# Chunk mask of the latent scores inside the contraction, and half as many mask columns for the differential scores

## The chip, the cores and the metric

The kernel runs on one core of one Trainium2 chip. The metric is the device time of one execution in microseconds. An execution is compared with others by the median of several runs.

## The reference

Two layers of a streaming encoder are run for a prompt (512 new frames) and for samples (8 streams of 16 new frames with 256 cached ones). Layer 0 has two groups of heads side by side, latent attention and differential attention; layer 1 has stick-breaking attention. Both head groups of layer 0 use the same chunk-causal mask: a frame sees all frames of its own chunk of 64 and of the chunks before.

```python
CHUNK = 64

def _chunk_mask(qpos, kpos):
    return (kpos[None, :] // CHUNK) <= (qpos[:, None] // CHUNK)

def _mla_core(q_abs, q_rope, ckv, krope, qpos, kpos):
    s = (einsum('bqhc,bkc->bhqk', q_abs, ckv) + einsum('bqhr,bkr->bhqk', q_rope, krope)).astype(float32)
    s = jnp.where(_chunk_mask(qpos, kpos), s * (MLA_QK_DIM ** -0.5), NEG_INF)
    p = jax.nn.softmax(s, axis=-1).astype(ckv.dtype)
    return jnp.einsum('bhqk,bkc->bqhc', p, ckv)

def _diff_core(q, k, v, qpos, kpos, lam):
    s = jnp.einsum('bqhid,bkhid->bhiqk', q, k).astype(jnp.float32) * (DIFF_HD ** -0.5)
    s = jnp.where(_chunk_mask(qpos, kpos), s, NEG_INF)
    p = jax.nn.softmax(s, axis=-1)
    a = (p[:, :, 0] - lam * p[:, :, 1]).astype(v.dtype)
    return jnp.einsum('bhqk,bkhe->bqhe', a, v)
```

## The kernel before

The prompt's 512 frames are four tiles of 128 rows, the samples are a fifth tile. All matrix products with the large weights are made of three products of split operands (a high and a low part). The weights come in quarters of 256 KB from SP's queue into a ring of three stages (`load_quarter`, L727); ScalarE writes the high part (`w_hi`, L1368), VectorE the low part (`w_lo`, L1598), and TensorE takes a quarter when both are there. SP issues the load of quarter n + 3 when quarter n has been split.

The order of the work is one list of jobs, `make_schedule`, written out by hand. Each engine runs through the same list and does its own part of each job; semaphores join them. A job that TensorE writes to PSUM takes a bank from a ring, and waits until the bank's last use has been read.

Behind the first projections comes the job `rms`: POOL and VectorE norm the latents, and POOL then issues the stores of the new latents and rotary keys: first those of the samples (L889, L890), then, when these have landed, those of the prompt (L892, L893). SP waits for the samples' stores and loads their latents back (L753). At this time the projection of the values `dv` is under way; SP, ScalarE and VectorE handle its weight quarters.

Then follow 48 steps of softmax attention: 16 latent steps ("M", tile t of the queries, pair of heads), 8 latent sample steps ("MS"), 16 differential steps ("D", tile t, head) and 8 differential sample steps ("DS"). Tile t of the queries sees key tiles 0 to t, so a score has 128, 256, 384 or 512 columns. A step makes two score maps side by side in two banks (`pair`); VectorE takes their row maxima (`peak`, L1699), ScalarE the exponential (L1448), VectorE the weights (L1720). Two steps later TensorE transposes the weights (`turn`, `turn2`), ScalarE and VectorE copy the result (L1469, L1735), and another step later TensorE makes the product with the values. Between these parts stand pieces of the next projections (`dk`, `dq` and so on) and, ahead of a sample's score, the transposes of its cache (`cacheT`, L1059 and L1061, copied by VectorE in L1690 and L1691).

In a latent step the contraction of a score runs over 96 rows: 64 rows that are the head's own and 32 rotary ones. Queries lie in `qT`, which is the memory of `x_sb` (the profile gives it that name), keys in `mlaK`. A fp32 product of TensorE appears as two matmuls. After the two scores, two bf16 matmuls add the mask to the last 128 columns of each map: the stationary operand is the unit matrix, the moving one is `mask_chunk`, with -1e30 where the key's chunk is a later one. The differential steps do the same. All tiles of 128 keys below the last one are fully visible, so only the last tile needs a mask; in it the rows of the first chunk must not see the second chunk's 64 columns.

```python
for i in range(2):
    h = 2 * pair + i
    mm(o[:, i, 0:n], qT[0:QK, h, tok(t)], mlaK[0:QK, h, 0:n], True, False)
for i in range(2):
    m = mm(o[:, i, n - P:n], identb[:, :], mask_chunk[:, :], False, True)
m.then_inc(done, 1)
```

Of the kernel before, what the change touches and what calls it, by code (L numbers as in the profile page):

```python
# [25 lines left out]
BF16 = mybir.dt.bfloat16  # L26
# [4 lines left out]
P = 128  # L31
# [13 lines left out]
EPS = 1e-5  # L45
MH, NOPE, ROT, MV = 8, 64, 32, 64
QK = NOPE + ROT
QL, KVL = 256, 128
SEC_A = QL + KVL + ROT
DH, HD, DROT = 4, 64, 16  # L50
# [364 lines left out]
def trunk_kernel(nc, a, out):  # L415
# [9 lines left out]
    def sem(name):  # L425
        return ctx.enter_context(nc.semaphore(name))
# [4 lines left out]
    with ctx:  # L431

        def sb(name, shape, dt=F32):
            return alloc(ctx, name, shape, dt)
# [10 lines left out]
        latT = work8[:, :, :].rearrange("p a b -> p (a b)")[:, 0:3 * TOK].rearrange("p (a b) -> p a b", a=3)  # L445
        ident = sb("ident", [P])
        identb = sb("identb", [P], BF16)
        mask_chunk = sb("mask_chunk", [P], BF16)
        mask_causal = sb("mask_causal", [P], BF16)
        mask_new = sb("mask_new", [NEW], BF16)  # L450
        peak = sb("peak", [8, 2])
# [102 lines left out]
        hi_done, cvt_done = sem("hi_done"), sem("cvt_done")  # L554
        pool_cvt_done = sem("pool_cvt_done")
        xhi_done = sem("xhi_done")
        upper_read = sem("upper_read")
        subln_done = sem("subln_done")
        ocvt_hi, ocvt_done = sem("ocvt_hi"), sem("ocvt_done")
# [305 lines left out]
        def _(pool):  # L865
# [17 lines left out]
            for job in schedule:  # L883
                kind = job[0]
                if kind == "rms":
                    pool.wait_ge(pow_in, pow_no[job])
                    nc.gpsimd.tensor_tensor(ss[:, 2, :], ss[:, 1, :], minus_half[:, :], ALU.pow).then_inc(pow_out, 1)
                    pool.wait_ge(rms_done, 1)
                    pool.dma_start(ckv_s, lat[:, S_TILE, QL:QL + KVL]).then_inc(stored_ckv, 16)  # L889
                    pool.dma_start(kr_s, lat[:, S_TILE, QL + KVL:]).then_inc(stored_ckv, 16)  # L890
                    pool.wait_ge(stored_ckv, 32)
                    pool.dma_start(ckv_p, lat[:, 0:PT_TILES, QL:QL + KVL]).then_inc(stored_ckv, 16)  # L892
                    pool.dma_start(kr_p, lat[:, 0:PT_TILES, QL + KVL:]).then_inc(stored_ckv, 16)  # L893
                elif kind == "dk":
                    _, t, half = job
                    n = rot_no[job]
                    pool.wait_ge(rot_done, n)
                    pool.dma_start((dk_p[t] if t < PT_TILES else dk_s)[:, half * HALF:(half + 1) * HALF],
                                   rot[:, (n - 1) % 4, :]).then_inc(stored_rot[(n - 1) % 4], 16)
                elif kind == "dv" and job[2] == 1:  # L900
                    t = job[1]
                    wait_drained(pool, ("dv", t, 0))
                    wait_drained(pool, job)
                    if t < PT_TILES:
                        outputs += 16
                        pool.dma_start(dv_p[t], dv[:, t, :]).then_inc(stored, 16)
                    else:
                        pool.dma_start(dv_s, dv[:, t, :]).then_inc(stored_dv, 16)
                elif kind == "post":
                    pool.wait_ge(pow_in, pow_no[job])  # L910
                    sums = sums_of(job[1])
                    nc.gpsimd.tensor_tensor(ss[:, 2, sums], ss[:, 1, sums], minus_half[:, 0:DH], ALU.pow).then_inc(pow_out, 1)
                elif kind == "cvt" and job[1] in POOL_SPLITS:
                    n = job[1]
                    sec, words = n // QUARTERS, slice(n % QUARTERS * 512, (n % QUARTERS + 1) * 512)
                    pool.wait_ge(hi_done, n + 1)
                    nc.gpsimd.tensor_tensor(w_lo[:, sec % 2, words], stage[:, n % STAGES, :],
                                            w_hi[:, sec % 2, words].bitcast(F32), ALU.subtract).then_inc(pool_cvt_done, 1)
                elif kind == "ln":
                    i = ln_no[job] % 2  # L920
                    pool.wait_ge(pow_in, pow_no[job])
                    if ln_no[job] > 2:
                        n = ln_no[job] - 2
                        pool.wait_ge(ln_done, n)
                    nc.gpsimd.tensor_tensor(rstd[:, i, :], mv[:, i, 1:2], minus_half[:, 0:1], ALU.pow).then_inc(pow_out, 1)  # L925
                elif kind in ("k", "v"):
                    _, g, t = job
                    wait_drained(pool, job)
                    cols = slice(g * GW, (g + 1) * GW)
                    k_out, v_out = (sk_p[t], sv_p[t]) if t < PT_TILES else (sk_s, sv_s)  # L930
                    if kind == "k":
                        slot = (kn_no[job] - 1) % 2
                        pool.dma_start(k_out[:, cols], k_n[:, slot, :]).then_inc(stored_kn[slot], 16)
                    else:
                        pool.dma_start(v_out[:, cols], v_n[:, g % 2, t, :]).then_inc(
                            stored_vn[g % 2] if t < PT_TILES else stored_v[g], 16)
# [13 lines left out]
        def _(pe):  # L950
# [45 lines left out]
            for job in schedule:  # L996
# [76 lines left out]
                elif kind == "score":  # L1073
# [4 lines left out]
                    if s[0] == "M":  # L1078
                        _, t, pair = s
                        pe.wait_ge(kr_done, PT_TILES)  # L1080
                        for j in range(4):
                            wait_drained(pe, ("latT", j))
                        for i in range(2):
# [1 line left out]
                            wait_drained(pe, ("qT", t, i))  # L1085
                        for i in range(2):
                            h = 2 * pair + i
                            mm(o[:, i, 0:n], qT[0:QK, h, tok(t)], mlaK[0:QK, h, 0:n], True, False)
                        for i in range(2):
                            m = mm(o[:, i, n - P:n], identb[:, :], mask_chunk[:, :], False, True)  # L1090
                        m.then_inc(done, 1)
                    elif s[0] == "MS":
                        b = s[1]
# [9 lines left out]
                    elif s[0] == "D":  # L1103
# [5 lines left out]
                            r = slice(HD * i, HD * i + HD)  # L1109
                            mm(o[:, i, 0:n], dqT[t][r, h, :], dkT[r, h, 0:n], True, False)  # L1110
                        for i in range(2):
                            m = mm(o[:, i, n - P:n], identb[:, :], mask_chunk[:, :], False, True)
                        m.then_inc(done, 1)
                    elif s[0] == "DS":
                        b = s[1]
# [451 lines left out]
        def _(dve):  # L1567
# [17 lines left out]
            for job in schedule:  # L1585
# [42 lines left out]
                elif kind == "lam":  # L1628
# [2 lines left out]

                    dve.wait_ge(consts_in, 16)
                    v.tensor_copy(identb[:, :], ident[:, :])
                    v.tensor_copy(mask_chunk[:, :], probs[:, 0, 0:P])
                    v.tensor_copy(mask_causal[:, :], probs[:, 0, P:2 * P])
                    v.tensor_copy(mask_new[:, :], probs[:, 0, 2 * P:MASKS])
                    link(v.tensor_tensor(lam4[:, 0:2, :], lam4[:, 0:2, :], lam4[:, 2:4, :], ALU.mult))
# [274 lines left out]
def shape_constants():  # L1912
# [1 line left out]
    r = np.arange(P)  # L1914
    neg = np.float32(-1e30)
    masks = np.zeros((P, MASKS), np.float32)
    masks[:, 0:P] = np.where(r[None, :] // 64 <= r[:, None] // 64, 0, neg)
    masks[:, P:2 * P] = np.where(r[None, :] < r[:, None], 0, neg)
    masks[:, 2 * P:] = np.where(r[None, :NEW] < r[:, None] % NEW, 0, neg)
    sel = ((r[:, None] // QUAD == r[None, :] // QUAD) & (r[:, None] % NEW == r[None, :] % NEW)).astype(np.float32)  # L1920
    second = r // NEW % 2
    sign = np.stack([1 - second, second], 1).astype(np.float32)
    pos = np.concatenate([np.arange(SEQ), PAST + r % NEW]).astype(np.float32)

    def rope(rot, theta):
# [3 lines left out]
        both = np.stack([np.cos(ang), np.cos(ang), -np.sin(ang), np.sin(ang)], 1).astype(np.float32)  # L1929
        return np.ascontiguousarray(both.reshape(TILES, P, 2, 2, half).transpose(1, 0, 2, 3, 4))  # L1930

    return {"c_ident": np.eye(P, dtype=np.float32), "c_masks": masks, "c_sel": sel, "c_sign": sign,
            "c_ropem": rope(ROT, 10000.0), "c_roped": rope(DROT, 500000.0)}


# [14 lines left out]
```

## Time and profile before

| | |
|---|---|
| median of 3 runs | 857.05 us (856.89 to 857.83) |
| the profiled execution's own time | 856.7 us |
| its span, first to last instruction | 854.9 us |
| TensorE (PE) busy, matmuls | 826.6 us, 97% |
| VectorE (DVE) busy | 524.8 us, 61% |
| ScalarE (ACT) busy | 412.8 us, 48% |
| GpSimd (POOL) busy | 74.8 us, 9% |
| TensorE's share of the chain that ended last | 81% |
| DMA, mean over the span | 101 GB/s |

Busy time counts the time in which an engine has at least one instruction running; matmuls overlap one another, so that the time from one start to the next says more than a matmul's duration. The chain that ended last is followed back from the last instruction, at each step to what released it. Loads of weights onto TensorE are a row of their own (PEld). A row of a view in order of time merges like instructions that follow one another: start, time from the first start to the last end, engine, line, operation, what is written and read, shapes, count, and in brackets the idle time before and who ended it. Since a window cuts such merges, a row's count can be that of a part.

### The profile page before, as it was taken

The page shows a single profiled execution, that of the slowest core. Times are in us where ns is not written, and L with a number is a line of the kernel's source. Part 1 is how long each engine was busy: PE and PEld are TensorE (multiplying, and loading weights), DVE is VectorE, ACT ScalarE, POOL GpSimd, SP SyncE. Part 2 cuts the span into 40 slices and gives each one's busy share as a digit, 9 for nine tenths or more (in the row PEclk, how much of TensorE's full clock was granted, in tenths as well). Part 3 has the DMA queues.
Part 4 walks back from the last instruction along what each step waited for, and adds up shares of the span by engine and source line. Part 5 has one row for each costly group of instructions (what it writes and reads, how often), then busy time and mean ns, then how long its engine had stood idle before and what let it go on. Part 6 is the DMA issues. An engine that isn't in the chain of part 4 may idle for free.

```text
span 854.9 us, 17106 instructions
## 1 busy us (share of the span) xinstructions
PE 826.6 (97%) x6676; PEld 706.4 (83%) x6676; DVE 524.8 (61%) x1048; ACT 412.8 (48%) x945; POOL 74.8 (9%) x102
## 2 busy tenths in 40 slices
PE   7999999999999999999999999999999999999995
PEld 6996688888888888768899998889888878887674
DVE  4175346655565647756942465666666766778777
ACT  4333433334354455532234556675566665687710
POOL 3020001000000000000220011001100110121002
PEclk9999999999999999999999999999999999999998
DMA  7631211211332334414133334233332433334113
GB/s 236 153 98 51 62 44 57 64 44 38 96 99 88 109 108 138 152 51 148 56 113 105 119 106 130 87 92 125 122 99 79 136 114 116 122 119 146 52 38 123
DMA packets 67534, 86.25 MB, mean 101 GB/s; under 512 B 6017, under 2 KB 53921, under 8 KB 67457
## 3 DMA queue, kind: packets, MB, share of 16 engines
q1 hardware_dynamic: 63712, 74.47, 28.4%
q0 software_dynamic: 3744, 10.70, 4.0%
q8 instruction: 55, 0.90, 0.4%
q14 instruction: 23, 0.18, 0.1%
HBM read 74.25 MB, written 10.90 MB: 100 GB/s over the span
## 4 chain that ended last, share of the span: by engine, by line
PE 81%; issue 9%; DVE 4%; ACT 4%; POOL 2%; DMA 0%; DVEq 0%; SPq 0%; POOLq 0%; ACTq 0%
PE turn L952 24%; PE pair L952 17%; PE value L952 16%; PE proj L952 15%; PE turn L992 3%; PE turn L1168 2%; POOL rstd L925 1%; PE value L992 1%; PE proj L992 1%; PE proj L1168 1%; DVE w_lo L1598 1%; ACT w_hi L1368 1%; PE pair L992 1%; DVE probs L1710 0%; PE value L1168 0%
## 5 line engine op out<-in xcount | busy, mean ns | idle before, releaser
L1598 DVE TENSOR_TENSOR w_lo<-stage,w_hi 128x512 fp32r<-128x512 f32 (+1 forms) x136 | 91.9, 683 | 118.2 <-ACT w_hi L1368 117.8
L952 PE MATMUL turn<-w_hi,xT_hi 128*128 128x256 f32 (+2 forms) x340 | 106.0, 312 | 0.9 <-DVE xT_lo L1603 0.6
L952 PE MATMUL turn<-w_hi,xT_lo 128*128 128x256 f32 (+2 forms) x340 | 102.5, 301 | 0.0
L952 PE MATMUL turn<-w_lo,xT_hi 128*128 128x256 f32 (+2 forms) x340 | 102.4, 301 | 0.0
L1368 ACT CAST w_hi<-stage 128x512 fp32r<-128x512 f32 (+1 forms) x144 | 87.4, 616 | 20.6 <-PE value L952 6.4
L952 PEld LDWEIGHTS turn<-w_hi,xT_hi 128*128 128x128 f32 x340 | 64.8, 191 | 3.6 <-DVE x_sb L1840 1.4
L952 PEld LDWEIGHTS turn<-w_hi,xT_lo 128*128 128x128 f32 x340 | 64.8, 191 | 2.4
L952 PEld LDWEIGHTS turn<-w_lo,xT_hi 128*128 128x128 f32 x340 | 64.9, 191 | 2.1
L1710 DVE TENSOR_TENSOR_SCAN probs<-probs 128x512 f32<-128x512 f32 (+4 forms) x80 | 61.5, 801 | 1.7
L1448 ACT ACTIVATE work<-pair,peak 128x512 f32<-128x512 f32 (+4 forms) x80 | 40.9, 516 | 44.5 <-DVE peak L1699 44.4
L952 PE MATMUL value<-w_hi,xT_hi 128*128 128x256 f32 (+2 forms) x194 | 60.5, 312 | 0.4 <-DVE w_lo L1598 0.4
L952 PE MATMUL value<-w_lo,xT_hi 128*128 128x256 f32 (+2 forms) x194 | 57.7, 297 | 0.0
L952 PE MATMUL value<-w_hi,xT_lo 128*128 128x256 f32 (+2 forms) x194 | 57.6, 297 | 0.0
L952 PE MATMUL proj<-w_hi,xT_hi 128*128 128x256 f32 (+2 forms) x186 | 56.1, 302 | 0.3
L952 PE MATMUL proj<-w_hi,xT_lo 128*128 128x256 f32 (+2 forms) x186 | 54.4, 293 | 0.0
L952 PE MATMUL proj<-w_lo,xT_hi 128*128 128x256 f32 (+2 forms) x186 | 54.4, 292 | 0.0
L952 PE MATMUL pair<-w_hi,xT_hi 128*128 128x256 f32 (+2 forms) x160 | 53.0, 331 | 0.1
L952 PE MATMUL pair<-w_hi,xT_lo 128*128 128x256 f32 (+2 forms) x160 | 52.0, 325 | 0.0
L952 PE MATMUL pair<-w_lo,xT_hi 128*128 128x256 f32 (+2 forms) x160 | 52.0, 325 | 0.0
L952 PE MATMUL turn<-xT_hi,w_hi 128*128 128x320 f32 x160 | 50.9, 318 | 0.0
L952 PE MATMUL turn<-xT_hi,w_lo 128*128 128x320 f32 x160 | 49.4, 309 | 0.0
L952 PE MATMUL turn<-xT_lo,w_hi 128*128 128x320 f32 x160 | 49.4, 309 | 0.0
(528 smaller groups left out, 2079.1 us busy)
## 6 DMA issues: line engine op xcount, KB each, us to landing
stage<-in_w_in_odd_dram SPq DMA_DIRECT2D x64, 256.0 KB, 2.7
stage<-in_w_in_even_dram SPq DMA_DIRECT2D x44, 256.0 KB, 2.8
k_c<-in_cache_sb_k_dram SPq DMA_DIRECT2D x32, 256.0 KB, 3.4
v_c<-in_cache_sb_v_dram SPq DMA_DIRECT2D x32, 256.0 KB, 2.9
mlaK<-in_cache_diff_k_dram SPq DMA_DIRECT2D x8, 512.0 KB, 4.1
mlaK<-in_cache_diff_v_dram SPq DMA_DIRECT2D x8, 512.0 KB, 4.3
stage<-in_w_out_even_dram SPq DMA_DIRECT2D x16, 256.0 KB, 2.6
stage<-in_w_out_odd_dram SPq DMA_DIRECT2D x16, 256.0 KB, 2.6
```

The source lines that it names most:

```text
L925: nc.gpsimd.tensor_tensor(rstd[:, i, :], mv[:, i, 1:2], minus_half[:, 0:1], ALU.pow).then_inc(pow_out, 1)
L952: return nc.tensor.matmul(o, l, r, start=first, stop=last)
L992: i = nc.tensor.transpose(ps(job)[0:c, c0:c0 + r], src, ident[0:r, 0:r])
L1168: m = nc.tensor.transpose(ps(job)[0:kn, j * P:(j + 1) * P], p[:, k0:k0 + kn], ident[:, :])
L1368: nc.scalar.copy(piece(w_hi[:, sec % 2, k * 512:(k + 1) * 512]), piece(stage[:, n % STAGES, :])).then_inc(hi_done, 1)
L1448: e = nc.scalar.activation(prob(s, i), ps(score)[:, i, 0:width(s)], ACT.Exp, bias=peak[:, r, i:i + 1], accum_out=total[:, r, i:i + 1])
L1598: v.tensor_tensor(piece(w_lo[:, sec % 2, words]), piece(stage[:, n % STAGES, :]), piece(w_hi[:, sec % 2, words].bitcast(F32)), ALU.subtrac ...
L1710: i = v.tensor_tensor_scan(c, c, c, 0.0, ALU.add, ALU.max)
```

## The change

The mask of the latent scores moves into the contraction. Eight rows are added to queries and keys, one for each chunk of the prompt: row c of the queries is 1 where the query's own chunk comes before chunk c, row c of the keys is -1e30 where the key lies in chunk c. Their product is -1e30 exactly where the key's chunk is a later one. The rows are constants (`c_chunks`, 2 x 8 x 512 words in DRAM) and are loaded on POOL's queue into partitions 96 to 103 of `qT` and `mlaK`, the same for all eight heads. The two mask matmuls of a latent step are gone, and each latent score waits for `chunks_in`.

The differential steps keep their two mask matmuls, which now add only the last 64 columns of the mask to the last 64 columns of the map; the 64 columns before them held zeros only.

```diff
+CHUNK = 64
+CHUNKS = SEQ // CHUNK
+QKM = QK + CHUNKS
...
-        mask_chunk = sb("mask_chunk", [P], BF16)
+        mask_chunk = sb("mask_chunk", [CHUNK], BF16)
...
+        chunks_in = sem("chunks_in")
...
                     pool.wait_ge(rms_done, 1)
+                    for i, rows in enumerate((qT[QK:QKM, :, 0:SEQ], mlaK[QK:QKM, :, :])):
+                        pool.dma_start(rows, a["c_chunks"][i].unsqueeze(1).broadcast_to([CHUNKS, MH, SEQ])).then_inc(chunks_in, 16)
                     pool.dma_start(ckv_s, lat[:, S_TILE, QL:QL + KVL]).then_inc(stored_ckv, 16)
...
                         pe.wait_ge(kr_done, PT_TILES)
+                        pe.wait_ge(chunks_in, 32)
...
                         for i in range(2):
                             h = 2 * pair + i
-                            mm(o[:, i, 0:n], qT[0:QK, h, tok(t)], mlaK[0:QK, h, 0:n], True, False)
-                        for i in range(2):
-                            m = mm(o[:, i, n - P:n], identb[:, :], mask_chunk[:, :], False, True)
+                            m = mm(o[:, i, 0:n], qT[0:QKM, h, tok(t)], mlaK[0:QKM, h, 0:n], True, True)
                         m.then_inc(done, 1)
...
                             mm(o[:, i, 0:n], dqT[t][r, h, :], dkT[r, h, 0:n], True, False)
                         for i in range(2):
-                            m = mm(o[:, i, n - P:n], identb[:, :], mask_chunk[:, :], False, True)
+                            m = mm(o[:, i, n - CHUNK:n], identb[:, :], mask_chunk[:, :], False, True)
...
-                    v.tensor_copy(mask_chunk[:, :], probs[:, 0, 0:P])
+                    v.tensor_copy(mask_chunk[:, :], probs[:, 0, P - CHUNK:P])
...
+    own, chunk = np.arange(SEQ)[None, :] // CHUNK, np.arange(CHUNKS)[:, None]
+    chunks = np.stack([np.where(own < chunk, 1, 0), np.where(own == chunk, neg, 0)]).astype(np.float32)
```

POOL's order at the job `rms`, before (`lat` holds the latents, `dv` the values):

```order
L887 TENSOR_TENSOR ss<-ss,minus_half 128x10 [waits pow_in]
L889 DMA out_dram<-lat 128x128 [waits rms_done]
L890 DMA out_dram<-lat 128x32
L892 DMA out_dram<-lat 128x4x128 [waits stored_ckv]
L893 DMA out_dram<-lat 128x4x32
```

and with the change:

```order
L891 TENSOR_TENSOR ss<-ss,minus_half 128x10 [waits pow_in]
L894 DMA x_sb<-in_c_chunks_dram 8x8x512 [waits rms_done]
L894 DMA mlaK<-in_c_chunks_dram 8x8x512
L895 DMA out_dram<-lat 128x128
L896 DMA out_dram<-lat 128x32
L898 DMA out_dram<-lat 128x4x128 [waits stored_ckv]
L899 DMA out_dram<-lat 128x4x32
```

Two DMAs stand ahead of the stores; nothing else of POOL's order moves.

TensorE's order at a latent step on tile 0 (`ckv_c` and `kr_c` are a sample's cache, `vm` the values), before:

```order
L1059 MATMUL value<-ident,ckv_c 128x128
L1061 MATMUL value<-ident,kr_c 96x128 x2
L952 MATMUL pair<-mlaK,x_sb 128x128 [waits drained_score0,drained_score1,drained_proj0,drained_turn0,drained_value0,drained_turn2,drained_turn1,kr_done,drained_pair1]
L952 MATMUL pair<-mlaK,x_sb 128x128
L952 MATMUL pair<-mask_chunk,identb 128x128 x2
L952 MATMUL proj<-probs,vm 64x128 [waits drained_proj0,drained_turn1,drained_value0]
L952 MATMUL proj<-probs,vm 64x128
```

and with the change:

```order
L1065 MATMUL value<-ident,ckv_c 128x128
L1067 MATMUL value<-ident,kr_c 96x128 x2
L958 MATMUL pair<-mlaK,x_sb 128x128 [waits drained_score0,drained_proj0,drained_score1,drained_value0,drained_turn0,drained_turn1,drained_turn2,chunks_in,kr_done,drained_pair1]
L958 MATMUL pair<-mlaK,x_sb 128x128
L958 MATMUL proj<-probs,vm 64x128 [waits drained_proj0,drained_turn1,drained_value0]
L958 MATMUL proj<-probs,vm 64x128
```

The mask's row is gone in each of the 16 latent steps, and each waits for `chunks_in` besides. In the differential steps the row stays and reads 128x64.

## Rows read from the trace of the kernel before

**Rows 1.** The page: busy us (share) x instructions; the chain that ended last by engine.
```profile
PE 826.6 (97%) x6676; PEld 706.4 (83%) x6676; DVE 524.8 (61%) x1048; ACT 412.8 (48%) x945; POOL 74.8 (9%) x102
...
PE 81%; issue 9%; DVE 4%; ACT 4%; POOL 2%; DMA 0%; DVEq 0%; SPq 0%; POOLq 0%; ACTq 0%
```

**Rows 2.** Stretches: us, busy PE PEld DVE ACT POOL (x), granted clock, DMA share, GB/s.
```profile
100.00:150.00 50.00, 48.19 (x345) 39.05 (x344) 24.63 (x71) 19.68 (x55) 3.78 (x7) 1.00 0.18 50
150.00:200.00 50.00, 49.31 (x373) 41.05 (x372) 29.04 (x84) 19.11 (x61) 1.62 (x3) 1.00 0.19 52
```

**Rows 3.** Instructions on mask_chunk: duration min/median/max, first and last start.
```profile
L952 PEld LDWEIGHTS pair<-mask_chunk,identb x64: 95/98/100, 105.4 to 371.5; 128*128 128x128 bf16 x64
L952 PE MATMUL pair<-mask_chunk,identb x64: 217/220/230, 105.8 to 371.5; 128*128 128x128 bf16 x64
```

**Rows 4.** TensorE in order of time: start us, us, what; a latent step, tile 2.
```profile
155.91 1.46 PE L952 MATMUL pair<-mlaK,x_sb 96*128 96x384 f32 x4
157.21 0.28 PE L952 MATMUL pair<-mask_chunk,identb 128*128 128x128 bf16 x2
157.41 1.09 PE L952 MATMUL value<-probs,vm 128*64 128x128 f32 x16
```

**Rows 5.** The same view where a narrow product follows transposes with no mask.
```profile
665.99 0.63 PE L992 MATMUL value<-ident,k_c 128*128 128x128 f32 x4
666.46 0.27 PE L992 MATMUL proj<-ident,oval 128*128 128x128 f32 x1
666.66 0.88 PE L952 MATMUL turn<-work,v_n 128*64 128x128 f32 x12
```

**Rows 6.** The same view of VectorE and TensorE, a latent step on tile 0.
```profile
148.67 0.42 DVE L1691 COPY lat<-value 32x256 f32<-32x256 f32 x1
...
147.25 0.28 PE L952 MATMUL pair<-mask_chunk,identb 128*128 128x128 bf16 x2
...
149.19 0.67 PE L952 MATMUL pair<-lat,w_uq 128*128 128x256 f32 x2 [0.38 <-issue]
```

**Rows 7.** The same view behind the first latent step on tile 2.
```profile
123.27 0.44 PE L952 MATMUL value<-probs,vm 128*64 128x128 f32 x4 [0.36 <-DVE probs L1735]
```

**Rows 8.** The same view, differential steps: the next product with 64, with 128 columns.
```profile
242.77 0.29 PE L952 MATMUL pair<-mask_chunk,identb 128*128 128x128 bf16 x2
242.99 0.66 PE L952 MATMUL value<-probs,vm 128*64 128x128 f32 x8
...
281.80 0.28 PE L952 MATMUL pair<-mask_chunk,identb 128*128 128x128 bf16 x2
281.92 1.11 PE L952 MATMUL value<-dv,probs 128*128 128x128 f32 x8
```

**Rows 9.** The same view of POOL, SP, ScalarE, VectorE and TensorE, 56 to 61 us.
```profile
56.02 0.62 POOL L889 DMA_DIRECT2D out_dram<-lat  x1 [5.77 <-DVE lat L1582]
...
56.35 4.61 SPq L727 DMA_DIRECT2D stage<-in_w_in_even_dram  x4
...
59.22 0.62 ACT L1368 CAST w_hi<-stage 128x512 fp32r<-128x512 f32 x1 [2.44 <-DMA stage<-in_w_in_even_dram]
...
59.88 0.69 DVE L1598 TENSOR_TENSOR w_lo<-stage,w_hi 128x512 fp32r<-128x512 f32 x1 [2.35 <-ACT w_hi L1368]
...
60.62 0.39 PE L952 MATMUL pair<-w_hi,xT_hi 128*128 128x256 f32 x1
```

**Rows 10.** DMA issues of the whole run: count, KB each, median us to landing.
```profile
stage<-in_w_in_even_dram SPq DMA_DIRECT2D x44, 256.0 KB, 2.8
...
ropem<-in_c_ropem_dram POOLq DMA_DIRECT2D x1, 160.0 KB, 2.5
...
g_q<-in_q_norm_g_dram POOLq DMA_DIRECT2D x1, 128.0 KB, 4.0
```

**Rows 11.** DMA queues and issues from 20 to 26 us.
```profile
q0 software_dynamic: 146, 0.38, 98.1%
...
stage<-in_w_in_even_dram SPq DMA_DIRECT2D x2, 256.0 KB, 10.4
```

More of the change, by code:

```diff
@@ L1916, in shape_constants @@
     masks = np.zeros((P, MASKS), np.float32)
-    masks[:, 0:P] = np.where(r[None, :] // 64 <= r[:, None] // 64, 0, neg)
+    masks[:, 0:P] = np.where(r[None, :] // CHUNK <= r[:, None] // CHUNK, 0, neg)
     masks[:, P:2 * P] = np.where(r[None, :] < r[:, None], 0, neg)
@@ L1930, in rope @@
         return np.ascontiguousarray(both.reshape(TILES, P, 2, 2, half).transpose(1, 0, 2, 3, 4))
-    return {"c_ident": np.eye(P, dtype=np.float32), "c_masks": masks, "c_sel": sel, "c_sign": sign,
+    return {"c_ident": np.eye(P, dtype=np.float32), "c_masks": masks, "c_chunks": chunks, "c_sel": sel, "c_sign": sign,
             "c_ropem": rope(ROT, 10000.0), "c_roped": rope(DROT, 500000.0)}
```

## The prediction

> **What bounds the kernel now.** I read the page first, then the stretch table, the mask's own instructions, and then short stretches of the order in time around one step of each kind. TensorE is busy for 97% of the span and carries 81% of the chain that ended last [rows 1]. In the stretches that hold most latent steps it is busy for 48.2 of 50 us, then 49.3 of 50, and its clock is granted in full [rows 2]. So time taken off TensorE there is time off the end, except just ahead of a place where TensorE waits for something that did not depend on it. Those exceptions decide this change. A difference under 0.2% (1.7 us) I count as no change, about what a measurement of this kernel can tell.
>
> **Part 1: the mask matmuls of the latent scores go.** There are 64 mask matmuls, 32 of them in the 16 latent steps [rows 3]. In a latent step the first mask matmul starts at 157.21 and the value product behind it at 157.41 [rows 4]: the pair costs 0.20 us from start to start. Not all of that comes back. The value product holds only 64 stationary columns, and where such a product follows a transpose with no mask between them, it starts 0.20 us after it (666.46 to 666.66) [rows 5], while the transposes ahead of it start about 0.12 us apart (four in 0.63 us, of which 0.27 is the last one's own time). So 0.09 us of the 0.20 is a price of the change of shape that stays, and a removed pair is worth 0.11 us. The bound above is 0.20, if the change of shape hides under the long score matmul.
>
> Where does the 0.11 us reach the end? Of a latent step on a query tile 3 or 2 the value product follows at once and TensorE goes on. Of a step on tile 0 or 1 it doesn't: between the masks and the next stall there are only a few short products. At 147.25 the masks of such a step run, and at 149.19 the sample's score starts after a wait; the last thing to come is VectorE's copy of the cache transposes, which ends at 149.09 [rows 6]. VectorE comes to it after a rotation and a weight split, and both wait for ScalarE's work on the projection before. All of that hangs on the projection that TensorE finished before the score, not on the masks. A TensorE that arrives 0.11 us sooner waits 0.11 us longer. I find such a stall behind seven of the eight steps on tiles 0 and 1; behind the eighth the copy ends about 0.1 us ahead of TensorE, which is no gain either. The first step on tile 2 is the same: its value product starts at 123.27 after 0.36 us idle that a copy on VectorE ended [rows 7]. That leaves seven of sixteen steps: 7 x 0.11 = 0.8 us. The bound above is 7 x 0.20 = 1.4.
>
> The eight added rows of the contraction cost nothing on TensorE: the stationary and moving columns stay as they are, and the four score matmuls of 384 columns start 0.32 us apart (1.30 us to the first mask) [rows 4], which is their columns twice at 2.4 GHz, and rows don't enter. Nor does the new wait at the first latent score, whose masks run at 105.8 us [rows 3]: its transfers are issued at about 56 us [rows 9], and weight quarters in the thickest traffic of the start landed in 10.4 us [rows 11].
>
> **Part 2: 64 mask columns in place of 128 for the differential scores.** All 32 mask matmuls stay, half as wide. Two of them last 0.28 us together where one lasts 0.22 [rows 3, 8], so the second starts 0.06 us after the first. Before a value product with 64 stationary columns the pair takes 0.22 us up to the next start (242.77 to 242.99), before one with 128 only 0.12 (281.80 to 281.92) [rows 8]. In the second case the next product's weights are what is late: its eight matmuls take 1.11 us with the last one's 0.27, so 0.84 for seven steps of 0.11, and the extra is the first weight load that the short mask cannot cover. There a narrower second mask brings nothing. Five of the sixteen steps are of the first kind. At least 5 x 0.03 = 0.15 us is gained, at most 16 x 0.06 = 1.0 (each mask costs half). I take 0.35, nearer the lower end, because weight loads of 0.10 us already stand behind each mask [rows 3]. The Trainium skill (TensorE: Matmul & The Clock Gate, section "Back-to-back issue gap") puts the floor of a matmul with up to 64 columns at about 25 ns; by it the first mask of each pair would fall from 0.06 to 0.03 us and the sum would gain 16 x 0.03 = 0.5 in place of 0.35. No row here has such a mask.
>
> VectorE's copy of the mask is one short instruction that gets half as long; it stands off the path, and I count nothing. The score reductions read the same columns as before.
>
> **Part 3: two DMAs are put ahead of the stores on POOL's queue.** They bring 8 x 8 x 512 words each, 128 KB into eight partitions, every 2 KB row read eight times. POOL would issue them at 56.02 and, 0.62 us later, at 56.64, where it now issues the two sample stores [rows 9]. Those stores move back by 1.2 us, and with them the two prompt stores, which wait for them, and SP's load of the new latents behind its four weight quarters. SP has no further quarter to load for a long while then, and VectorE asks for the prompt stores only at the first cache transposes, behind the first latent score: nothing of this is late.
>
> What is late next is a weight quarter. SP issues four quarters from 56.35 on [rows 9]. The first of them is the last quarter of the second value section. It lands just before 59.22, where ScalarE, idle for 2.44 us on that DMA, converts it; VectorE follows at 59.88 after 2.35 us idle, and TensorE, which reaches the product with this quarter at 60.62, finds it ready with nothing to spare [rows 9]. Behind it on ScalarE stand the four copies of the rotary keys, behind them VectorE's latent copies, and for those TensorE's key products wait. So each microsecond by which this quarter lands later is a microsecond at the end. It shares the DMA engines with the two new transfers, which are issued 0.3 us before it and 0.3 after.
>
> The price of that is in no row of the trace; the nearest bound it. Below: nothing, if they pass on engines that the quarter doesn't need. As ordinary traffic: a load of 160 KB lands in 2.5 us and one of 256 KB in 2.8 [rows 10], 0.3 us for 96 KB, so 256 KB more in the way are 0.8. Above: at the start POOL loads gains and lambdas as rows that all 128 partitions read from one place. In the stretch from 20 to 26 us POOL's queue filled 98.1% of all engines with 0.38 MB, 64 GB/s, and the weight quarters issued then landed after 10.4 us [rows 11]. At that rate 256 KB take 4.1 us. One 128 KB transfer of that kind landed in 4.0 us, a plain one of 160 KB in 2.5 [rows 10], so 1.5 us more for its repeated reads. The new rows are repeated 8 times, not 128, and are read from eight places. I take 1.5 us, nearest to the pair of 128 and 160 KB.
>
> **The sum.** -0.8 (latent masks) - 0.35 (half-wide masks) + 1.5 (the late quarter) = +0.35 us. Against the profiled execution's 856.7 us that is 857.05. The median of the runs shown is 857.05, 0.35 above that execution, so the forecast for the median is 857.4 us: no change that can be measured. With a late quarter of 0.4 to 2.9 us it is 856.3 to 858.8.
>
> **The rivals.**
> *The new transfers clog the engines.* Mechanism: eight partitions and repeated rows make them slow, and the quarter waits behind them. Price: 4.1 us by the start's rate, so 857.05 - 1.15 + 4.1 = 860.0, slower. It decides from 2.9 us on. For it: the idle ScalarE and the 98.1% with 64 GB/s. Against it: few engines may be involved, and the repetition is 8, not 128. The Trainium skill (SBUF — State Buffer, section "Door 1: The DMA port swizzle") says that DMA bandwidth goes with the ports that the partitions reach, and partitions 96 to 103 reach two of sixteen, at some 27 GB/s each. As an estimate from that page the two transfers would take 4.8 us, and if the quarter waited for all of it the time would be 860.7. No row of this trace shows so narrow a large transfer.
>
> *The transfers cost nothing.* Then only the gains are left: 855.9 by my terms, 854.65 with both upper ends (1.4 and 1.0). It is faster by more than 1.7 us only if the masks are worth over 1.7 us, so for most of this case's width it is still no change. For it: the 2.8 us landing is mostly latency.
>
> *The change gives its full count on TensorE.* If the stalls behind the tile 0 and 1 steps shrank too, 16 x 0.11 + 0.5 = 2.3 us would go, and with a quarter that is late by 0.5 us the time is 855.25. Against it: the order in time at 147 to 149 us, where ScalarE and VectorE never wait for a mask.
>
> **How the numbers follow.** The forecast has 0.40, the clog 0.36, free transfers 0.17, the full count 0.07. Of the last two I give 0.17 to faster by over 0.2%, the rest is within it; the clog is all slower but for its lower edge. So faster 0.17, same 0.48, slower 0.35. The range for 8 in 10 goes from 855.0, inside the free case, to 860.0, the clog's own value.
>
> **What would show it.** The mask should have 32 matmuls of 64 columns, and value products should start one score matmul plus 0.09 us after the last score's start. The stalls that now end at 149.19 should be 0.1 us longer. ScalarE's conversion at 59.22 should move to about 60.7, and everything after it until the first latent score with it. The forecast is wrong if that conversion stays where it is and the first latent score still starts at 104 us after the same launch, or if it moves past 62. My split of the gain is wrong if TensorE is more than 1.5 us ahead between the first latent score and 375 us.

## The result and the profile after

The changed kernel takes 861.74 us in the median of 6 runs (861.06 to 862.06), the kernel before, run beside it, 857.44 (856.40 to 859.91). The ratio is 1.0050, 95% interval 1.0040 to 1.0061: slower by 0.5%, 4.3 us. The forecast was 857.4 with a range up to 860.0. The profiled execution took 861.52 us, with a span of 859.7 against 854.9.

The page: busy us by engine, and the chain of waits by engine.
```profile
PE 825.6 (96%) x6644; PEld 704.5 (82%) x6644; DVE 524.6 (61%) x1048; ACT 413.0 (48%) x945; POOL 76.0 (9%) x104
...
PE 78%; issue 9%; DVE 6%; ACT 4%; POOL 2%; DMA 1%; SPq 0%; DVEq 0%; POOLq 0%; ACTq 0%
```
TensorE is busy for 1.0 us less than in [rows 1], and the span is 4.8 us longer: the loss is waiting, and the chain has lost 3% of TensorE for 2% of VectorE and 1% of DMA. The stretch table shows where. The kernel before (columns as in [rows 2]):
```profile
56.00:61.00 5.00, 5.00 (x45) 4.88 (x44) 2.25 (x5) 2.13 (x4) 2.48 (x4) 1.00 0.59 174
61.00:75.00 14.00, 13.92 (x63) 8.21 (x62) 10.06 (x28) 5.71 (x12) 0.74 (x2) 1.00 0.21 64
```
and the changed one:
```profile
56.00:61.00 5.00, 5.00 (x46) 5.00 (x46) 2.17 (x5) 0.37 (x1) 2.36 (x4) 1.00 0.64 89
61.00:75.00 14.00, 9.88 (x30) 5.30 (x28) 8.16 (x24) 6.15 (x10) 2.08 (x3) 0.88 0.50 113
66.00:67.00 1.00, 1.00 (x7) 1.00 (x7) 0.65 (x2) 1.00 (x2) 0.84 (x2) 0.50 0.44 44
```
Between 61 and 75 us TensorE is busy for 9.88 us where it had 13.92, and its clock is granted at 0.88 on average, at 0.50 from 66 to 67 us; in no other stretch up to 600 us does its busy time differ by more than 0.8 us. The order in time, of POOL, SP, ScalarE, VectorE and TensorE:
```profile
56.70 0.64 POOL L894 DMA_DIRECT2D x_sb<-in_c_chunks_dram  x1 [5.78 <-DVE lat L1587]
...
57.03 8.82 SPq L731 DMA_DIRECT2D stage<-in_w_in_even_dram  x4
...
57.34 0.58 POOL L894 DMA_DIRECT2D mlaK<-in_c_chunks_dram  x1
...
57.90 0.60 POOL L895 DMA_DIRECT2D out_dram<-lat  x1
...
64.11 0.62 ACT L1373 CAST w_hi<-stage 128x512 fp32r<-128x512 f32 x1 [6.65 <-DMA stage<-in_w_in_even_dram]
...
64.76 0.69 DVE L1603 TENSOR_TENSOR w_lo<-stage,w_hi 128x512 fp32r<-128x512 f32 x1 [6.55 <-ACT w_hi L1373]
...
65.51 0.58 PE L958 MATMUL pair<-w_hi,xT_hi 128*128 128x256 f32 x1 [4.12 <-DVE w_lo L1603]
...
66.10 0.41 PE L958 MATMUL pair<-w_hi,xT_lo 128*128 128x256 f32 x1
...
66.32 0.41 PE L958 MATMUL pair<-w_hi,xT_hi 128*128 128x256 f32 x1
```
This execution reached POOL's first issue at 56.70, 0.68 us later than [rows 9]; that lateness is there already at VectorE's split of x early in the launch (15.00 against 14.33) and is not the change's. Counted from POOL's first issue, ScalarE's conversion comes 7.41 us later where it came after 3.20: **4.21 us late**. TensorE stood idle for 4.12 us for it. Then it runs its matmuls of 256 columns 0.21 us apart instead of 0.12, the lower of its two clock levels (1.2 GHz) in place of 2.4 GHz. From this first matmul behind the wait to the first one on `work` and `w_uk` it needs 3.89 us in the kernel before and 4.94 in the changed one. The first latent score in the order in time, of the kernel before:
```profile
103.98 1.98 PE L952 MATMUL pair<-mlaK,x_sb 96*128 96x512 f32 x4 [0.70 <-ACT vm L1411]
```
and of the changed one:
```profile
109.91 1.98 PE L958 MATMUL pair<-mlaK,x_sb 104*128 104x512 f32 x4 [0.70 <-ACT vm L1416]
```
From POOL's first issue that is 47.96 us before and 53.21 now, **5.25 us later**: 4.21 of the late quarter, 1.04 at the lower clock. The landings say why (POOL's and SP's issues from 56 to 61 us, median us to landing; in the kernel before the quarters of this stretch had 3.0, of the whole run 2.8 [rows 10]):
```profile
stage<-in_w_in_even_dram SPq DMA_DIRECT2D x3, 256.0 KB, 7.2
x_sb<-in_c_chunks_dram POOLq DMA_DIRECT2D x1, 128.0 KB, 6.4
mlaK<-in_c_chunks_dram POOLq DMA_DIRECT2D x1, 128.0 KB, 7.0
```
The two sample stores behind them were held up as well: 7.2 and 7.4 us to landing.

The gains of the masks are there too. The masks that are left, by their duration in ns:
```profile
L958 PE MATMUL pair<-mask_chunk,identb x32: 193/198/203, 242.1 to 376.1; 128*128 128x64 bf16 x32
```
TensorE in order of time: a stall as [rows 6] showed it at 149.19, a latent step as in [rows 4], and two differential steps as in [rows 8]:
```profile
154.88 0.67 PE L958 MATMUL pair<-lat,w_uq 128*128 128x256 f32 x2 [0.49 <-issue]
...
161.61 1.46 PE L958 MATMUL pair<-mlaK,x_sb 104*128 104x384 f32 x4
162.99 1.09 PE L958 MATMUL value<-probs,vm 128*64 128x128 f32 x16
...
247.81 0.23 PE L958 MATMUL pair<-mask_chunk,identb 128*128 128x64 bf16 x2
247.97 0.66 PE L958 MATMUL value<-probs,vm 128*64 128x128 f32 x8
...
286.71 0.23 PE L958 MATMUL pair<-mask_chunk,identb 128*128 128x64 bf16 x2
286.78 1.14 PE L958 MATMUL value<-dv,probs 128*128 128x128 f32 x8
```
The value product stands 1.38 us behind the first of four score matmuls that are 0.32 us apart: one score and 0.09 us more, as forecast. The stall has 0.49 us idle where it had 0.38: the 0.11 us freed ahead of it is waited away. A differential pair of masks takes 0.16 us up to the next product, and 0.07 where that product has 128 columns. From the first latent score to the first differential one it was 131.97 us and is 131.14 (**-0.83**); from there to the last matmul of the last differential score 135.29 and 134.82 (**-0.47**); behind that to the last matmul nothing changed (0.02 us). 5.25 - 0.83 - 0.47 = 3.95 us; with the 0.68 of the launch that is 4.6 of the 4.8 us between the spans. The medians are 4.3 us apart.

### The profile page after: what moved, and what is told of

Its sections match the earlier page's. It is cut to its first block, busy times and chain, and to the rows that moved or that the text cites. A ratio compares the mean times of both kernels' runs of the same rounds, so it can differ in the third digit from the quotient of the medians.

```text
span 859.7 us, 17046 instructions
## 1 busy us (share of the span) xinstructions
PE 825.6 (96%) x6644; PEld 704.5 (82%) x6644; DVE 524.6 (61%) x1048; ACT 413.0 (48%) x945; POOL 76.0 (9%) x104
## 4 chain that ended last, share of the span: by engine, by line
PE 78%; issue 9%; DVE 6%; ACT 4%; POOL 2%; DMA 1%; SPq 0%; DVEq 0%; POOLq 0%; ACTq 0%
PE turn L958 23%; PE value L958 16%; PE pair L958 15%; PE proj L958 15%; PE turn L998 3%; PE turn L1173 2%; POOL rstd L931 1%; PE value L998 1%; PE proj L998 1%; DMA stage<-in_w_in_even_dram 1%; DVE w_lo L1603 1%; ACT w_hi L1373 1%; PE proj L1173 1%; DMA x_sb<-in_x_prompt_dram 0%; DVE probs L1715 0%
```

## The experiments

Theory A: the loss is the two transfers, by way of one weight quarter and the clock. Theory B: it comes from using the rows (a wait, 104 rows of contraction). Eleven kernels ran: four on where the time goes, seven on when and why the transfers cost. "Late" is counted from POOL's first issue behind the norm (where no row transfer goes first, from the sample store) to ScalarE's conversion and to the first latent score, against 3.20 and 47.96 us in the kernel before.

**The transfers alone, nobody reads them.**
```diff
                     pool.wait_ge(rms_done, 1)
+                    for i, rows in enumerate((qT[QK:QKM, :, 0:SEQ], mlaK[QK:QKM, :, :])):
+                        pool.dma_start(rows, a["c_chunks"][i].unsqueeze(1).broadcast_to([CHUNKS, MH, SEQ])).then_inc(chunks_in, 16)
```


> The kernel before with only the two row transfers added at the changed kernel's place on POOL's queue; the masks stay as matmuls and the rows are read by nobody. Theory A (the transfers hold up the last quarter of the second value section, TensorE stands still for about 4 us, and its clock then falls for a while): slower by 4.5 to 5.5 us against the kernel before, ScalarE's conversion 4 to 5 us later than before (counted from the same point of the launch), a granted clock under 1.00 between 61 and 75 us. Theory B (the loss comes from using the rows: the wait of the first latent score, 104 rows of contraction in place of 96): within 0.5 us of the kernel before.

Measured: 863.44 us, ratio 1.0067 (1.0054 to 1.0080). ScalarE's conversion and TensorE's first matmul behind it, in order of time:
```profile
64.14 0.62 ACT L1375 CAST w_hi<-stage 128x512 fp32r<-128x512 f32 x1 [6.51 <-DMA stage<-in_w_in_even_dram]
...
65.54 0.58 PE L959 MATMUL pair<-w_hi,xT_hi 128*128 128x256 f32 x1 [3.98 <-DVE w_lo L1605]
```
The conversion is 4.06 us late, TensorE idle for 3.98, the first latent score 5.02 late. The transfers by themselves make the whole loss; theory B falls. The time is 5.8 us longer by the ratio, 6.1 by the medians, somewhat over the 4.5 to 5.5 that theory A had.

**The same rows, loaded at three other moments.** Early: ahead of the wait for the norm. Late: behind the first store of differential values. Behind: just behind the two sample stores.
```diff
+                    for i, rows in enumerate(...):            # early
                     pool.wait_ge(rms_done, 1)
-                    for i, rows in enumerate(...):            # as changed
                     pool.dma_start(ckv_s, ...)
                     pool.dma_start(kr_s, ...)
+                    for i, rows in enumerate(...):            # behind
...
                         pool.dma_start(dv_p[t], dv[:, t, :]).then_inc(stored, 16)
+                        if outputs == 16:
+                            for i, rows in enumerate(...):    # late
```


> The changed kernel with the two row transfers issued ahead of POOL's wait for the norm, at about 51 us in place of 56, where the DMA engines of the kernel before are idle. Theory A: the loss goes almost wholly and the gains of the masks (0.8 and 0.4 us) stay: 0.5 to 1.5 us faster than the kernel before; the two transfers alone need some 6 to 7 us, so up to 1 us of the late quarter may be left. Theory B: 3.5 to 4.5 us slower than the kernel before, as the changed kernel is.

> The changed kernel with the two row transfers issued behind the first store of differential values, at about 69 us, with the first latent score at 104 us. Theory A: 1.0 to 1.4 us faster than the kernel before, no idle stretch of TensorE between 56 and 64 us, and the transfers land by 76 us, just as SP issues its next weight quarter. If the next quarters at 76 us are held up, TensorE has some slack there and the time rises by less than 1 us. Theory B: 3.5 to 4.5 us slower than the kernel before.

> The changed kernel with the two row transfers issued behind the two sample stores instead of ahead of them, 1.2 us later, so 0.9 and 1.5 us behind the issue of the weight quarter (which landed 2.8 us after its issue before). If the transfers must be in the engines first to hold it up: the quarter comes 0 to 1.5 us late and the time is at or just under that of the kernel before. If the quarter's own packets come out slowly and share with them to its end: 2 to 4 us late and 1.5 to 3.5 us slower than the kernel before.

Measured: early 856.05 us, ratio 0.9985 (0.9976 to 0.9994); late 856.12, 0.9984 (0.9975 to 0.9993); behind 855.58, 0.9984 (0.9973 to 0.9994). All three beat the kernel before by 0.15%, some 1.3 us, and can't be told from each other. The early kernel, the stretch in which its transfers now pass:
```profile
50.00:56.00 6.00, 6.00 (x52) 6.00 (x52) 5.40 (x8) 1.78 (x4) 1.65 (x3) 1.00 0.36 44
```
Its conversion:
```profile
59.46 0.62 ACT L1373 CAST w_hi<-stage 128x512 fp32r<-128x512 f32 x1 [2.46 <-DMA stage<-in_w_in_even_dram]
```
Its first latent score:
```profile
104.18 1.98 PE L958 MATMUL pair<-mlaK,x_sb 104*128 104x512 f32 x4 [0.70 <-ACT vm L1416]
```
And the conversion of the kernel with the rows behind the stores:
```profile
60.38 0.62 ACT L1373 CAST w_hi<-stage 128x512 fp32r<-128x512 f32 x1 [2.38 <-DMA stage<-in_w_in_even_dram]
```
Early the transfers take 5.5 and 5.8 us to land and are all but done when the quarter is issued at 56.6; late they are issued at 65.5 and 66.1 (the expectation had about 69) and pass between two weight loads, and the quarters issued from 76 us on are not disturbed (2.9 us to landing); behind they are issued 1.2 us later than in the changed kernel, and the quarter is not late at all (0.06 us ahead). The expectation of 0 to 1.5 us late holds at its lower end; the one of packets that share to the end fails. Traffic is heavy there all the same (a DMA share of 0.52 from 61 to 75 us, where the kernel before has 0.21); it falls on transfers that nobody waits for. What counts is what goes in ahead of the quarter or right beside it: the changed kernel's second transfer is issued 0.31 us behind it, this kernel's first one 0.82 us behind. No run sends only one of the two, so their shares in the delay are not shown.

**Only the differential masks.**
```diff
                         for i in range(2):
-                            m = mm(o[:, i, n - P:n], identb[:, :], mask_chunk[:, :], False, True)
+                            m = mm(o[:, i, n - P // 2:n], identb[:, :], mask_chunk[:, P // 2:], False, True)
```


> The kernel before with only the differential masks made half as wide; the latent scores keep their mask matmuls of 128 columns and no transfer is added. The sum of the prediction had 0.35 us for it, bounds 0.15 and 1.0; the two traces show 0.4 us between the first and the last differential score. Expected: 0.4 us faster, which may not be told from nothing; in the trace, 0.4 us less between the first and last differential score, and no difference before it.

Measured: 856.58 us, ratio 0.9989 (0.9980 to 0.9998). The first differential score:
```profile
235.94 1.13 PE L952 MATMUL pair<-dkT,x_sb 64*128 64x512 f32 x4
```
and the last masks:
```profile
370.93 0.23 PE L952 MATMUL pair<-mask_chunk,identb 128*128 128x64 bf16 x2
```
That is 134.99 us; the kernel before has 235.95 and 371.44, 135.49: 0.50 us gained, and nothing before it. The interval reaches from 0.2 to 1.7 us.

**What makes the transfers slow: width, repeated reads, bytes.** The kernel before, with other transfers at the same place, read by nobody. (In the wide one ScalarE also waits for them before it writes `vm`, at about 103 us, when they have long landed.)
```diff
+    pool.dma_start(vm[:, i, 0:2 * P], a["c_chunks"][i])                     # wide, x2: 128 partitions, 1 KB each
+    pool.dma_start(rows, a["c_chunks"][i])                                  # full, x2: source 8 x 8 x 512, read once
+    pool.dma_start(rows_of_head_0, a["c_chunks"][i])                        # small, x2: 16 KB
```


> The kernel before with two transfers of 128 KB at the changed kernel's place, of the same bytes but to all 128 partitions (1 KB each) and from a plain source of zeros; they are read by nobody. Theory N (the width of eight partitions is what makes the transfers hold up the weight quarter): at most 1.5 us slower than the kernel before, conversion at most 1.2 us later. Theory R (it is the bytes, or the place in the queues): 4 to 6 us slower, as with the narrow transfers.

> The kernel before with the two narrow transfers, but from a source of 8 x 8 x 512 words in which each row stands eight times, so that nothing is read twice. Theory N: as slow as with repeated reads, 5 to 6 us over the kernel before, conversion 4 to 5 us later. Theory P (the repeated reads of one place are the cost, as the prediction took for its 1.5 us): at most 2 us slower.

> The kernel before with the two narrow transfers cut to one head each, 16 KB into eight partitions. By bytes (theories N and R alike): an eighth of the delay, about 0.5 us or less. If the place in the queue alone were the cost (two more issues ahead of the stores, whatever their size): 4 us or more.

Measured: wide 858.19 us, ratio 1.0010 (1.0001 to 1.0020); full 861.97, 1.0048 (1.0032 to 1.0065); small 857.51, 1.0001 (0.9992 to 1.0010). TensorE's wait for the quarter with the wide transfers:
```profile
61.49 0.39 PE L959 MATMUL pair<-w_hi,xT_hi 128*128 128x256 f32 x1 [0.54 <-DVE w_lo L1606]
```
and with the full source:
```profile
64.33 0.39 PE L959 MATMUL pair<-w_hi,xT_hi 128*128 128x256 f32 x1 [3.08 <-DVE w_lo L1605]
```
The same 256 KB to all partitions cost 0.6 us, and with no repeated read the narrow ones still 3.2 of 4.1: it is the width. (Theory N had set the full source at 4 to 5 us late; with 3.18 it falls short of that. In run time it is 4.1 us slower by the ratio, 5.2 by the medians, where N had 5 to 6 and P at most 2.) The repeated reads are at most the 0.9 us between (the row lengths differ too). 32 KB cost nothing, and so do two issues ahead of the stores.

**Narrow in partitions, or in ways into the memory.** 128 and 64 KB from a plain source to eight partitions, neighbours, 16 apart, or 4 apart; the rest is the same. (ScalarE also waits for them before it writes that memory, first at about 76 us, when they have landed for more than 10 us.)
```diff
+    pool.dma_start(flat(x_sb)[S, 0:4096], a["c_chunks"][0])            # S: QK:QKM, 8:P:16 or 0:32:4
+    pool.dma_start(flat(vm)[S, 0:2048], a["c_chunks"][1][:, 0:2048])
```


> The kernel before with a transfer of 128 KB and one of 64 KB (16 KB and 8 KB for a partition) into eight neighbouring partitions, 96 to 103, from a plain source of zeros, at the changed kernel's place. Three quarters of the bytes of the narrow pair whose conversion came 3.2 us late. Both theories: conversion 1.8 to 3 us later than before, 2 to 4 us slower.

> The same two transfers with the same packets, into eight partitions that lie 16 apart (8, 24, ... 120). Theory S (neighbouring partitions share a way into the memory, as the page on SBUF's ports in the Trainium skill has it, and that is what is full): conversion at most 0.8 us later than before, at most 1 us slower. Theory C (few partitions, or few and long rows, are slow wherever they lie): as late as with neighbouring partitions, within 0.5 us.

> The same two transfers once more, with the same packets, into eight partitions that lie 4 apart (0, 4, ... 28). The conversion came 2.9 us late with neighbouring partitions and 1.5 us late with partitions 16 apart. Theory S, as a rule of ways into the memory (the Trainium skill, SBUF — State Buffer, section Door 1: The DMA port swizzle: partitions 96 to 103 reach two ports, eight partitions 16 apart from 8 on reach four, eight 4 apart reach eight): half of the last again, 0.6 to 0.9 us late, 0.5 to 1.5 us slower. Theory D (what counts is how far apart the partitions lie): as late as neighbours or between the two, 1.6 to 3 us. Theory E (half of the delay belongs to the eight long rows, wherever they lie): 1.3 to 1.7 us late.

Measured: neighbours 862.19 us, ratio 1.0064 (1.0049 to 1.0079); 16 apart 859.73, 1.0045 (1.0031 to 1.0059), its runs from 858.07 to 861.80, of which the profiled one is the lowest; 4 apart 857.35, 1.0005 (0.9995 to 1.0014). With neighbours, TensorE's wait:
```profile
63.38 0.39 PE L959 MATMUL pair<-w_hi,xT_hi 128*128 128x256 f32 x1 [2.83 <-DVE w_lo L1612]
```
and the stretch with its clock, then two parts of it:
```profile
61.00:75.00 14.00, 11.62 (x30) 5.48 (x30) 9.40 (x27) 6.63 (x11) 2.08 (x3) 0.88 0.37 94
63.00:64.00 1.00, 0.62 (x5) 0.62 (x6) 0.60 (x2) 1.00 (x2) 0.00 (x0) 0.99 0.33 114
64.00:65.00 1.00, 1.00 (x5) 0.76 (x4) 0.65 (x2) 1.00 (x2) 0.40 (x1) 0.50 0.48 79
```
With partitions 16 apart, the same two:
```profile
61.73 0.39 PE L959 MATMUL pair<-w_hi,xT_hi 128*128 128x256 f32 x1 [1.43 <-DVE w_lo L1612]
```
and:
```profile
61.00:75.00 14.00, 13.19 (x54) 7.48 (x55) 10.76 (x29) 5.99 (x10) 2.07 (x3) 1.00 0.22 68
```
With partitions 4 apart ScalarE's conversion, 3.72 us behind POOL's first issue at 56.41:
```profile
60.13 0.62 ACT L1375 CAST w_hi<-stage 128x512 fp32r<-128x512 f32 x1 [2.95 <-DMA stage<-in_w_in_even_dram]
```
With equal packets and eight partitions each time, the quarter is 2.92, 1.53 and 0.52 us late, and the 128 KB transfer itself lands after 4.9, 4.0 and 3.1 us. The Trainium skill (SBUF — State Buffer, section "Door 1: The DMA port swizzle") gives these three sets two, four and eight ports. The trace agrees: the first doubling of ports about halves the delay, the second does better. Theory S had put partitions 16 apart at 0.8 us at most, as if spreading alone freed them; their four ports go with the 1.53. The step from four to eight ports was forecast at 0.6 to 0.9 us late and 0.5 to 1.5 slower, and came at 0.52 and 0.4. Theory C (as late as neighbours) fails, distance alone (theory D) fails, since 4 apart is better than 16 apart, and long rows as such (theory E) fail too. Neighbours cost 5.5 us of run time where both theories had 2 to 4. One profile of each kernel was read: the step from eight ports to four shows in the run times too (857.35 and 859.73 us), while the intervals of four and two ports overlap, so that the size of this step rests on one execution each. Which of the DMA engines carried the packets no view tells.

| kernel | transfers | conversion late | first latent score late | median us | before, beside it |
|---|---|---|---|---|---|
| changed | 8 neighbours, repeated | 4.21 | 5.25 | 861.74 | 857.44 |
| transfers alone | the same | 4.06 | 5.02 | 863.44 | 857.33 |
| full | 8 neighbours, plain | 3.18 | 4.44 | 861.97 | 856.81 |
| neighbours | the same, 3/4 of the bytes | 2.92 | 4.28 | 862.19 | 856.56 |
| 16 apart | 3/4 of the bytes | 1.53 | 1.53 | 859.73 | 856.56 |
| wide | 128 partitions | 0.63 | 0.63 | 858.19 | 856.81 |
| 4 apart | 3/4 of the bytes | 0.52 | 0.51 | 857.35 | 856.93 |
| small | 32 KB in all | -0.02 | 0.00 | 857.51 | 856.81 |
| behind | as changed, 1.2 us later | -0.06 | -0.10 | 855.58 | 856.81 |
| early | as changed, 5.8 us earlier | 0.02 | -0.02 | 856.05 | 857.33 |
| late | as changed, 9.2 us later | 0.12 | 0.10 | 856.12 | 857.33 |

In the kernels whose quarter comes over 0.6 us late the medians stand 0.3 to 1.6 us above what their profiled execution's delay explains (changed 4.3 against 3.95, transfers alone 6.1 against 5.02, 16 apart 3.2 against 1.53). One profile each was read, and in 16 apart the runs themselves differ by 3.7 us; whether the quarter is later in other executions, or the launch, stays open.

## Why the prediction was wrong

**The step that failed is the price of the late quarter in part 3: "I take 1.5 us, nearest to the pair of 128 and 160 KB".** It measured 4.21 us. The path was as forecast, in each link: the quarter that ScalarE, VectorE and TensorE wait for, with nothing to spare, and everything to the first latent score behind it. The prediction's own sign of being wrong, a conversion past 62 us, came true: 64.11, or 63.43 without the launch's 0.68. The size was taken from transfers of like bytes and scaled down by repetition (8 against 128); repetition was the small part (at most 0.9 us), the two ways into the memory the large one. So the clog rival is what happened, by the first of the two reasons that it named, eight partitions and repeated rows. The prediction held the rule that says so, in that rival, and gave the case 0.36 since no row showed a narrow transfer. That the rival's own 4.1 us came within 0.1 of the measured delay is luck: it is the rate of repeated reads into all 128 partitions, 64 GB/s at the start [rows 11], and it leaves out the narrow destination.

**A term was missing: the clock.** No case counted that TensorE's clock falls around a wait of 4 us. It cost 1.04 us here. With it the clog's 860.0 would have been 861.0; the range, which ended at that rival's bare value, would have reached there, still 0.7 short of the measured 861.74. Of these 0.7, 0.4 is the kernel before, whose median over six runs is 857.44 and not 857.05. The estimate from the skill's page, 4.8 us and 860.7, lacked the clock as well.

**Part 1 was right, in size and in place.** Forecast -0.8, measured -0.83. Of the sixteen latent steps exactly seven became shorter, by 0.11 us each: the first, and those on tiles 3 and 2 behind the first tile 2. The other nine kept their length to 0.01 us, since the stall that follows grew by what the masks gave. The change of shape keeps 0.09 us. The full-count rival is out. The rows of the contraction and the new wait cost nothing, as said: the score matmuls are 0.32 us apart with 104 rows as with 96.

**Part 2 was a little low.** Forecast -0.35, measured -0.47 and -0.50 (0.15 to 1.0 allowed). From start to start the first mask of a pair went from 0.066 to 0.038 us, the second from 0.149 to 0.124 before a narrow product and from 0.056 to 0.029 before a wide one. "There a narrower second mask brings nothing" held: what the mask gives, 0.027, the wide product takes back, 1.14 us where it took 1.11 [rows 8], as its weights are late in turn. Such a step gains the 0.03 of its first mask, a narrow one 0.05. What was taken too low is the first mask: the forecast let the weight loads hold back part of its half, and 0.028 of its 0.066 us went in all sixteen steps. From one differential score to the next, thirteen of the fifteen steps between them are shorter by 0.05 to 0.06 (narrow) and 0.03 (wide); one wide step is not shorter at all and one narrow one by 0.02, which holds the sum at 0.47. The Trainium skill (TensorE: Matmul & The Clock Gate, section "Back-to-back issue gap") led to 0.5 in the prediction. The traces agree in the sum, -0.47 and -0.50; the first mask's 0.038 us stays above the page's floor of about 0.025.

**Part 3's other claims held in effect.** The stores and SP's load of new latents moved back with no wait on the path. But the prompt stores moved by 5.8 us and not by 1.2 (66.16 against 59.68, less the launch's 0.68), since the sample stores that they wait for were themselves held up. The free-transfer rival is what the early, late and behind kernels are: 1.3 us faster, between its 855.9 and 854.65 against 857.05.

## What to carry to other kernels

A rewrite that takes work off the bounding engine can lose to the loading of its constants: find the transfer that is waited for with nothing to spare, and issue no large narrow transfer just ahead of it: 192 to 256 KB into eight neighbouring partitions cost 2.9 to 4.2 us, the same bytes spread over more of the memory's ports 0.5 to 0.6, and 32 KB nothing. The same rows issued 1.2 us later, or in an idle stretch of the DMA engines, turn 4.3 us of loss into 1.3 us of gain. When an operand comes late to TensorE, add what the clock costs: 1.0 to 1.4 us with waits of 2.8 us and more here, nothing with 1.4.

## What the runs showed of the hardware

- Two transfers of 128 KB into eight neighbouring partitions, issued 0.6 us apart, landed after 5.5 and 5.8 us where nothing else passed (early), after 6.4 and 7.0 in the changed kernel; two of 128 KB into 128 partitions in 3.2. Transfers of the same 192 KB delayed a weight quarter issued 0.3 us behind the first of them by 2.92, 1.53 and 0.52 us on two, four and eight ports.
- In the kernels where TensorE was idle for 4.12, 3.98, 3.08 and 2.83 us the granted clock fell to 0.50 (0.88 on average from 61 to 75 us), at a cost of 1.04, 0.96, 1.26 and 1.36 us. The shorter waits cost more: behind 4.12 and 3.98 us the clock was down already when TensorE took up work, 0.3 and 0.5 us before; behind 3.08 and 2.83 its first matmuls still ran at the full level, and the clock fell 0.4 and 0.6 us later. With 1.43 and 0.54 us idle the stretch stayed at 1.00 and nothing more was lost.
- The instruction behind a mask matmul of 64 columns starts 0.03 to 0.04 us after it, where one of 128 took 0.06 to 0.07, if it is another mask or a product with 128 stationary columns (0.12 and 0.15 us before one with 64). Of the 0.055 us that a pair saves, 0.03 is left where a product with 128 columns follows.
